# One decoder layer on one core: every second routed block fetched as quarter rows and transposed by VectorE instead of TensorE

## What is computed

```python
def body(acc, blk):                     # blk: 128 tokens that go to expert e, their weights
    toks, bw, e = blk
    xb = hp[toks]                       # hp: the 2048 rows, and a row of zeros for padding
    yb = (jax.nn.silu(xb @ w_gate[e]) * (xb @ w_up[e])) @ w_down[e]
    return acc.at[toks].add(yb.astype(f32) * bw[:, None]), None
```

## Time and profile before

| | us |
|---|---|
| median of 3 runs | 2494.95 |
| lowest, highest run | 2492.94, 2497.22 |
| the profiled execution, its own time | 2485.66 |
| its span (first to last instruction) | 2483.8 |
| TensorE busy in the span | 2382.5 (96%) |
| VectorE, ScalarE, GpSimd busy | 1575.5, 1161.9, 767.3 |
| mean granted TensorE clock | 0.985 |

### The profile page before, as it was taken

The page is one execution under the profiler, slowest core; times in us unless marked ns, Lnnn a source line. Parts: engine busy times, 40 slices in busy tenths (PEclk is TensorE's granted clock), DMA queues, the critical chain, the costliest instruction groups (busy, mean ns, idle before and its releaser), DMA issues. The chain is left out here.

```text
span 2483.8 us, 49979 instructions
## 1 busy us (share of the span) xinstructions
PE 2382.5 (96%) x11840; PEld 1954.7 (79%) x11842; DVE 1575.5 (63%) x2285; ACT 1161.9 (47%) x1621; POOL 767.3 (31%) x829
## 2 busy tenths in 40 slices
PE   8899999989997799999999999999999999999986
PEld 6677777678886688888888888888888888888875
DVE  6686867768878756555665555656665556655447
ACT  4525253542225645445554445545554445544334
POOL 0010100011110134334543433534443334444327
PEclk9999999989998899999999999999999999999998
DMA  7242323364445579778988878888888789987863
GB/s 254 77 144 98 111 94 111 117 218 164 171 164 206 196 230 284 223 219 270 273 259 233 254 218 263 268 266 262 257 253 243 224 223 274 283 247 222 216 221 136
DMA packets 253808, 524.34 MB, mean 211 GB/s; under 512 B 18065, under 2 KB 165169, under 8 KB 249649
## 3 DMA queue, kind: packets, MB, share of 16 engines
q1 hardware_dynamic: 204464, 336.64, 39.7%
q0 software_dynamic: 48672, 186.86, 29.4%
q10 hardware_dynamic: 608, 0.02, 0.0%
HBM read 386.61 MB, written 136.87 MB: 211 GB/s over the span
## 5 line engine op out<-in xcount | busy, mean ns | idle before, releaser
L2503 PE MATMUL psG<-gu_split,xT_hi 128*128 x2624 | 624.3, 390 | 2.9 <-ACT xT_hi L2340 1.5
L2503 PEld LDWEIGHTS psG<-gu_split,xT_hi 128*128 128x128 f32 x2624 | 493.8, 188 | 106.2 <-issue 3.6
L2326 POOL DMA_INDIRECT acc<-y,si x162 | 290.1, 1791 | 728.6 <-DMA acc<-y,si 413.3
L2409 DVE TENSOR_TENSOR gu_split<-raw_gu,gu_split (+1 forms) x127 | 290.6, 2288 | 175.3 <-ACT gu_split L2344 171.7
L2514 PE MATMUL psG<-gu_split,xT_lo 128*128 x1304 | 339.3, 402 | 5.9 <-issue 5.8
L2514 PEld LDWEIGHTS psG<-gu_split,xT_lo 128*128 128x128 f32 x1304 | 233.1, 188 | 50.1 <-issue 8.7
L2344 ACT ACTIVATE gu_split<-raw_gu x126 | 234.3, 1907 | 33.5 <-issue 33.5
L2301 POOL DMA_INDIRECT xg<-htab,gi x164 | 205.0, 1250 | 130.4 <-POOL gi L2298 109.7
L2409 DVE TENSOR_TENSOR d_lo<-raw_d,d_hi (+1 forms) x64 | 146.7, 2292 | 149.5 <-ACT d_hi L2344 149.5
L2389 ACT ACTIVATE HT_hi<-psH 128x256 fp32r<-128x256 f32 x162 | 62.4, 385 | 351.6 <-PE psH L2521 351.6
L2406 DVE TENSOR_TENSOR xT_lo<-psX,xT_hi 128x512 fp32r<-128x512 f32 x328 | 209.7, 680 | 8.5 <-ACT xT_hi L2340 8.5
(11 more groups left out here) (388 smaller groups left out, 3723.7 us busy)
## 6 DMA issues: line engine op xcount, KB each, us to landing
raw_gu<-in_w_gate_dram SPq DMA_DIRECT2D x64, 1024.0 KB, 6.0
raw_gu<-in_w_up_dram SPq DMA_DIRECT2D x64, 1024.0 KB
raw_d<-in_w_down_dram SPq DMA_DIRECT2D x64, 1024.0 KB, 6.9
wring<-split_d SPq DMA_DIRECT2D x24, 1024.0 KB, 4.8
split_d<-wring POOLq DMA_DIRECT2D x8, 1024.0 KB, 4.2
raw_d<-mixed SPq DMA_DIRECT2D x16, 512.0 KB, 3.9
xt<-in_x_dram SPq DMA_DIRECT2D x16, 512.0 KB, 4.3
htab<-h SPq DMA_DIRECT2D x16, 512.0 KB, 2.6
```

The lines of the kernel that those rows point to most:

```text
L2326: nc.gpsimd.indirect_dma_start(out=acc, out_offset=bass.IndirectOffsetOnAxis(ap=si[k][:, 0:1], axis=0), in_=y[k][:], in_offset=None, compu ...
L2409: nc.vector.tensor_tensor(dst, src, hi, ALU.subtract).then_inc(dlo_s if n == 2 else gulo_s, 1)
L2503: nc.tensor.matmul(psG[slot][:], xT_hi[slot][:, c, :], right[:, bass.ds(w, 1), c, :].rearrange("p a n -> p (a n)"), start=(n == 0 and c == ...
```

## The change

Blocks with an even number go the old way, through one row gather and 8 TensorE transposes. Blocks with an odd number go a new way.

- A second table `hcut` in HBM holds the same rows cut in four pieces of `PIECE` = 272 values (256 features, 16 expert weights; 1088 bytes). `output_and_route` writes both tables: one more store of 512 KB per tile, and for each pair of tiles two more stores of weights in runs of 64 bytes; `place_and_share` writes 4 more stores of zeros. Waits on these stores count them (32 for 16, 48 for 16).
- An odd block is gathered by 4 indirect DMAs of 128 pieces each, so that partitions 32a to 32a+31 hold piece a. The piece numbers `pidx` come from 16 new small VectorE instructions in `indices`.
- VectorE turns the block in squares of 32x32 with two instructions (128x1024 and 128x128) into `xF` in SBUF. ScalarE and VectorE take the high and low part from there in one instruction each instead of two. The expert weights of the block are turned once more by one TensorE transpose (`turn_weights`) into `psW`, from which `pairw` is copied.
- Chunk c now holds features 8q+c for both kinds of blocks. Gate and up weights are loaded to match, and TensorE's transposes of even blocks read `xg` with a step of 8 values (32 bytes) between columns.
- The copies into `gi` and `si` move from GpSimd to ScalarE (`gather_index`, `scatter_index`).

The diff, cut to its core:

```diff
             def store_h(n):
                 sp.wait_ge(h_s, n + 1)
                 sp.dma_start(htab[n * P:(n + 1) * P, 0:D], h[n % 2][:]).then_inc(row_out[n % 2], 16)
+                sp.dma_start(hcut[n * P:(n + 1) * P, :, 0:FEATS], h[n % 2][:].rearrange("p (a w) -> p a w", a=QUADS)).then_inc(row_out[n % 2], 16)
...
+                for i in range(w):
+                    sp.dma_start(hcut[(t + i) * P:(t + i + 1) * P, :, FEATS:PIECE],
+                                 wrow[r % 2][:, i, :].rearrange("p (a e) -> p a e", a=QUADS)).then_inc(wt_out[r % 2], 16)
...
+def gather_pieces(nc, hcut, to, at, done):
+    for g in range(QUADS):
+        nc.gpsimd.indirect_dma_start(out=to[:, g, 0:PIECE], out_offset=None, in_=hcut.rearrange("r a w -> (r a) w"),
+                                     in_offset=bass.IndirectOffsetOnAxis(ap=at[:, g:g + 1], axis=0)).then_inc(done, 16)
...
+                dve.wait_ge(idx_s, 2)
+                odd = idx[:].rearrange("p (b k) -> p b k", k=2)[:, :, 1]
+                for a in range(QUADS):
+                    for g in range(QUADS):
+                        last = nc.vector.tensor_scalar(pidx[a * QP:(a + 1) * QP, :, g], odd[g * QP:(g + 1) * QP], float(QUADS), float(a),
+                                                       ALU.mult, ALU.add)
+                last.then_inc(idx_s, 1)
...
-                        sp.dma_start(dst, w[0, bass.ds(e, 1)].rearrange("a (k p) n -> p (a k) n", p=P)).then_inc(sm, 16)
+                        rows = "a (k p) n -> p (a k) n" if sm is down_in else "a (p k) n -> p (a k) n"
+                        sp.dma_start(dst, w[0, bass.ds(e, 1)].rearrange(rows, p=P)).then_inc(sm, 16)
...
                 for n, s, k in steps(i):
-                    pool.wait_ge(turned[1], s.n + 3)
-                    pool.wait_ge(pairw_s, s.n + 3)
+                    pool.wait_ge(next_gi_s, s.n + 1)
+                    if k == 0:
+                        pool.wait_ge(pairw_s[0], s.turn + 2)
                     carry_wait(pool, passed)
-                    gather(s.n + AHEAD, k, s.n + AHEAD + 1)
-                    nc.gpsimd.tensor_copy(si[k][:], idx[:, bass.ds(s.n, 1)]).then_inc(si_s, 1)
+                    if k:
+                        gather_pieces(nc, hcut, xg[1], gi[1], x_in[1])
+                    else:
+                        gather_rows(nc, htab, xg[0], gi[0], x_in[0])
...
+            def turn_x(nth):
+                dve.wait_ge(x_in[1], nth * 16 * QUADS)
+                if not (isinstance(nth, int) and nth == 1):
+                    dve.wait_ge(odd_wturn, nth - 1)
+                    dve.wait_ge(odd_xhi, nth - 1)
+                carry_wait(dve, passed)
+                nc.vector.transpose(xF[:, 0:KC, :].rearrange("p c (g j) -> p c g j", g=QUADS),
+                                    xg[1][:, :, 0:FEATS].rearrange("p g (i c) -> p c g i", c=KC))
+                nc.vector.transpose(xF[:, KC, :].rearrange("p (g j) -> p g j", g=QUADS),
+                                    xg[1][:, :, FEATS:WIDE]).then_inc(odd_turned, 1)
...
                     s.wait(dve, H_s)
-                    pair_weight(nexts[n + 1], k, s.turn + 2)
-                    product(s.n + 2, 1 - k)
+                    if k == 0:
+                        pair_weight(nexts[n + 1], s.turn + 2, 0)
+                        pair_weight(nexts[n], s.turn + 1, 1)
+                    product(s.n + 2, 1 - k, s.turn + 1 + k)
+                    if k == 0:
+                        turn_x(s.turn + 2)
                     when_first(dve, nexts[n + 1], lambda: split(nexts[n + 1], 0))
...
+                rows = xg[0][:, 0:D].rearrange("p (q c) -> p c q", c=KC)
                 for h in range(2):
+                    if not (isinstance(nth, int) and nth == 1):
+                        pe.wait_ge(xlo_s[h], nth - 1)
+                    for c in range(HALF):
+                        m = nc.tensor.transpose(psX[h][:, c, :], rows[:, h * HALF + c], ident[:])
+                    m.then_inc(turned[h], 1)
...
                     turn_H(1 - k)
-                    pe.wait_ge(x_in[1 - k], (s.turn + k + 2) * 16 )
-                    carry_wait(pe, passed)
-                    for h in range(2):
-                        pe.wait_ge(xlo_s[h], s.n + 3)
-                        turn_x(1 - k, h)
+                    if k:
+                        turn_weights(s.turn + 2)
+                        turn_x(s.turn + 3)
...
+            def high_x(nth, slot):
+                if slot:
+                    act.wait_ge(odd_turned, nth)
+                    nc.scalar.activation(xT_hi[1][:], xF[:, 0:KC, :], ACT.Copy).then_inc(odd_xhi, 1)
+                    return
```

More of the change, by code:

```diff
@@ L2175, in experts @@
         xlo_s = [sem(f"xlo_s{i}") for i in range(2)]
-        pairw_s = sem("pairw_s")
+        odd_turned = sem("odd_turned")
+        odd_wturn = sem("odd_wturn")
+        odd_xhi = sem("odd_xhi")
+        odd_xlo = sem("odd_xlo")
+        next_gi_s = sem("next_gi_s")
+        pairw_s = [sem(f"pairw_s{i}") for i in range(2)]
         dhi_s = sem("dhi_s")
@@ L2206, in expert, with column @@
                 return within(self.word & (EXPERTS - 1), 0, EXPERTS - 1)
+            def column(self):
+                share = EXPERTS // QUADS
+                return within((self.word & (EXPERTS - 1)) + (self.word & (EXPERTS - share)), 0, P - 1)
             def next(self):
@@ L2296, in _ @@
         def _(pool):
[L2297 to L2307 removed]
+            for k in range(2):
+                if k == 0:
+                    pool.wait_ge(turned[1], 1)
+                    pool.wait_ge(pairw_s[0], 1)
+                    nc.gpsimd.tensor_copy(gi[0][:], idx[:, 2:3]).then_inc(gi_s, 1)
+                    pool.wait_ge(gi_s, 3)
+                    gather_rows(nc, htab, xg[0], gi[0], x_in[0])
+                else:
+                    pool.wait_ge(odd_turned, 1)
+                    nc.gpsimd.tensor_copy(gi[1][:], pidx[:, 1, :]).then_inc(gi_s, 1)
+                    pool.wait_ge(gi_s, 4)
+                    gather_pieces(nc, hcut, xg[1], gi[1], x_in[1])
             for k in range(2):
@@ L2446, in _ @@
             split_first(1)
-            for h in range(2):
-                evac_x(h, 1, 0)
+            low_x(1, 0)
             split_first(2)
-            pair_weight(block0, 0, 1)
-            pair_weight(block1, 1, 1)
+            for k in range(2):
+                dve.wait_ge(acc_out[k], 16 * EARLY // 2)
+            pair_weight(block0, 1, 0)
+            dve.wait_ge(tails_s, 1)
+            turn_x(1)
             when_first(dve, block0, lambda: split(block0, 0))
-            product(1, 0)
-            for h in range(2):
-                evac_x(h, 2, 1)
+            product(1, 0, 1)
+            low_x(1, 1)
             when_first(dve, block0, lambda: split(block0, 1))
@@ L2483, in _, with turn_x, turn_weights, gate_up_high @@
         def _(pe):
-            def turn_x(slot, half):
-                for c in range(HALF):
-                    m = nc.tensor.transpose(psX[half][:, c, :], xg[slot][:, (half * HALF + c) * P:(half * HALF + c + 1) * P], ident[:])
-                m.then_inc(turned[half], 1)
-            def gate_up_high(nth, slot, entry):
-                for h in range(2):
-                    pe.wait_ge(xhi_s[h], nth)
+            def turn_x(nth):
+                pe.wait_ge(x_in[0], nth * 16)
+                carry_wait(pe, passed)
+                rows = xg[0][:, 0:D].rearrange("p (q c) -> p c q", c=KC)
+                for h in range(2):
+                    if not (isinstance(nth, int) and nth == 1):
[3 more added lines that the diff above has]
+                    m.then_inc(turned[h], 1)
+            def turn_weights(nth):
+                pe.wait_ge(odd_turned, nth)
+                if not (isinstance(nth, int) and nth == 1):
+                    pe.wait_ge(pairw_s[1], nth - 1)
+                carry_wait(pe, passed)
+                nc.tensor.transpose(psW[:], xF[:, KC, :], ident[:]).then_inc(odd_wturn, 1)
+            def gate_up_high(nth, slot, entry, seen):
+                if slot:
+                    pe.wait_ge(odd_xhi, seen)
+                else:
+                    for h in range(2):
+                        pe.wait_ge(xhi_s[h], seen)
                 pe.wait_ge(gulo_s, entry.rank() * 2)
@@ L2505, in gate_up_high, with gate_up_low @@
                                          start=(n == 0 and c == 0), stop=False)
-            def gate_up_low(nth, slot, entry):
-                for h in range(2):
-                    pe.wait_ge(xlo_s[h], nth)
+            def gate_up_low(nth, slot, entry, seen):
+                if slot:
+                    pe.wait_ge(odd_xlo, seen)
+                else:
+                    for h in range(2):
+                        pe.wait_ge(xlo_s[h], seen)
                 w = entry.slot()
```

175 lines of the change are left out of this document (100 added, 75 removed).

## The result

The change made the kernel slower: 2598.93 us (median of 4 runs, 2595.07 to 2603.21) against 2493.94 for the kernel before on the same chip (2487.02 to 2497.22). The ratio is 1.0425, 95% interval 1.0396 to 1.0454. The prediction was 2452, range 2435 to 2512.

The account below looks back on a forecast made before the run. TensorE's own work was taken as the bound, transfers second. 57 us saved less charges of 5, 3, 3 and 3 gave 43 off 2485.66: 2442.7, or 2452 as the median of runs; range 2435 to 2512.

Parts of the forecast that it names:

- What goes: TensorE in odd blocks: 8 transposes go, one comes; 0.70 us a turn, 57 us over 81 turns.
- the charges of 5, 3 and 3: Expected losses in the loop: 5 us for H's shorter cover, 3 for quarter gathers, 3 for denser transfers.
- The strided read: TensorE's weight loads in even blocks, step of 32 bytes: taken as no change; upper end 0.80 us more a block.
- its rival: Strided weight loads in even blocks run at half rate: 65 us back, 2517 us, range 2495 to 2530; chance 0.17.
- VectorE's turns: VectorE's transposition of odd blocks: 1.5 us, upper end 3.0, fitting into 2.77 us of idle time; cost nothing.
- The shorter cover for H: After even steps TensorE reaches the down product 0.80 us sooner and may wait for `HT_lo`; 5 us charged.
- Transfers and small packets: Transfer engines in the expert stage: pieces of 1088 bytes add 0.16 us of share a turn, taken as nothing.
- The rival of dear packets: Small indirect packets in odd blocks' gathers cost as large ones: 165 us slower, 2660 us; chance 0.04.
- ScalarE's copies: Two tiny index copies a step on ScalarE, 0.2 us each: nothing; without cover 65 us.
- Before the loop: Second-table stores, weight stores and index instructions ahead of the expert loop: 3 us in sum, bounds 1 and 6.
- Quarter gathers: GpSimd's four piece gathers in odd blocks: not the bound, pieces in time with about 1 us spare; 3 us charged.
- late pieces: VectorE waits for pieces behind stretched issues and a lagging scatter chain: 2503 us at worst, 2480 middle; chance 0.12.

Follow-up runs that it names:

- both: The changed kernel with one gather of whole rows for odd blocks and VectorE's transposition reading runs of 32 values: 2449.86 us, ratio 0.9837.
- layout: The kernel before with gate and up weights in the new feature order and TensorE's transposes of all blocks reading columns 32 bytes apart: 2490.6 us, ratio 1.0006.
- apart: The changed kernel with odd blocks' scatters into a second table and no scatter waiting for the one before: 2464.86 us, ratio 0.9903.
- four_short: The changed kernel with an odd block's four gathers fetching 32 whole rows each instead of 128 quarter rows: 2617.11 us, ratio 1.0518.
- tables: The kernel before with the stores into `hcut` and their waits added, and nothing that reads it: 2494.05 us, ratio 1.0024.
- one_gather: The changed kernel with an odd block fetched by one indirect DMA of 128 whole rows instead of four of quarter rows: 2462.3 us, ratio 0.9887.
- copies: The kernel before with only the copies of `gi` and `si` moved to ScalarE: 2485.87 us, ratio 0.999.
- spread: The changed kernel with two of the four pieces issued in the even step ahead of its scatter, two in the odd step: 2503.08 us, ratio 1.006.
- early: The changed kernel with all four pieces issued in the even step, ahead of its scatter: 2594.31 us, ratio 1.0436.
- spread_contig: The changed kernel with two pieces issued in each step and VectorE's transposition reading runs of 32 values: 2491.08 us, ratio 1.001.

## Why the prediction was wrong

**What goes: right.** With the four issues out of the way and VectorE's read contiguous (the kernel both) the loop is 42.8 us shorter; 57 less the charges of 5, 3 and 3 inside the loop was 46, though one of the 3 was for the quarter gathers, which that kernel doesn't have. The transposes start as foretold: eight at 1516.44, low matmuls at 1517.26, 0.82 us later, for 0.80 in the earlier trace rows.

**The strided read: right, and its rival refuted.** The weight load itself did get longer, 193 ns in place of 140 (first the changed kernel's, then the one before's; shortest, median, longest):

```profile
L2592 PEld LDWEIGHTS psX<-ident,xg x664: 185/193/230, 863.5 to 2495.2; 128*128 128x128 f32 x166
```

```profile
L2487 PEld LDWEIGHTS psX<-ident,xg x1320: 138/140/231, 852.8 to 2383.8; 128*128 128x128 f32 x189
```

but eight transposes still pass in 0.82 us, and layout, where every block's weight load takes 193 ns, stands at 1.0006. The same stride on VectorE costs 74%, 2.16 us for 1.24. The Trainium skill (Advanced Engine Details and Errata, SBUF Cachelines) says that another line for each access costs a penalty, without a size. Both lengths agree with it: here it is 0.05 us a load on TensorE, hidden, and 0.9 us an instruction on VectorE, not hidden.

**VectorE's turns at nothing: mis-sized.** 2.16 + 0.27 = 2.4 us lay between the 1.5 taken and the upper end of 3.0, but the 2.77 us of idle time didn't cover them in every turn. 0.91 us less in each turn gave 12 us with one gather or spread pieces and 24 in the changed kernel.

**The shorter cover for H: a little low.** 5 us was the charge. TensorE never waited for `HT_lo` before; it waits 7.5 us in 9 waits in the kernel both, 16.8 in 21 in apart and 21.5 in 28 in the changed kernel.

**Transfers and small packets: nothing, as taken.** The rival of dear packets fell with four_short and with a DMA share that fell to 0.82. ScalarE's copies cost nothing, as taken.

**Before the loop: perhaps mis-sized.** 3 us, at most 6, was the charge. The second table alone costs 1 to 11 us of the median (tables). The profiles can't size it better: the loop begins 11.9 us later in the changed kernel, 2.1 in one_gather, which does the same ahead of it but for its row numbers, and 7.0 in copies, which has neither table nor index instructions. Those are 0.25 us each, over 4.4 us.

**Quarter gathers: the step that failed.** "GpSimd issues 5 gathers and 2 scatters a turn: 5 x 1.25 + 2 x 1.79 = 9.8 us of 17.9, so it isn't the bound" took GpSimd's busy time for its hold on the turn. Three things in it were off.

First, the run of four. The prediction took 4 x 1.01 = 4.0 us. From the start of the first piece to the end of the fourth it is 4.7 us undisturbed and 6.0 on the mean (67 runs from 1000 to 2350 us), up to 8.3. Each issue is followed by 0.30 us, and one beside a VectorE split takes 2 to 3 us in place of 0.95: the fourth piece at 1515.88 took 3.05 beside a split from 1515.81, the first two of the next turn 3.01 and 2.45 beside those from 1531.49 and 1534.30. The prediction had the row for this and charged 3 us. In those 67 runs 56 of the 268 pieces took more than 1.8 us, and all 56 ran beside a VectorE instruction with two SBUF inputs, a split or the low part of an odd block; of the other 212 34 did. The Trainium skill's note that GpSimd contends with VectorE instructions of two SBUF inputs (GPSIMD Engine Reference, Key points) agrees with this trace.

Second, the landing. It took 3 to 4 us; the piece in the timeline took 5.7, the one case that was looked at.

Third, and this is the cause that apart shows, the scatters. 413 us of GpSimd waiting for its own scatters was read as a sign that GpSimd has time to spare. But a scatter that waits for the landing of the one before is part of a loop of its own, and in the kernel before about half of the scatters were released by it, on the mean 9.77 us after the one before, where a step took 9.34. There was little room, and TensorE's saving of 0.35 us a step could be had only if this loop got shorter too. It could, as the kernel both shows with 9.0 us and the wait in place. Instead each turn put four issues into one of its two links: the even scatter waits for a landing, the pieces wait behind it in GpSimd's order and so come late to VectorE, and the odd scatter waits behind the pieces or for a landing that has itself become later. In the changed kernel's trace a turn is so 10.44 + 9.63 = 20.1 us for 18.7. Take away the landing's wait (apart) or halve the run (spread), and 134 or 96 us come back. Move the run as a whole (early), and nothing does. Of the 147 us between the forecast of 2452 and the 2598.93 measured, 134 so hang on the wait and the run of four together: taking away either is enough (apart 134, one_gather 137), and apart's 2464.86 lies within the predicted range. VectorE's step, worth 12 us from one_gather to both and from spread to spread_contig, is the size of what is left, though the two weren't joined in one run.

The rival "late pieces" named the right queue and the "lagging scatter chain", but priced it as lateness against VectorE's deadline, 1 us in two of three turns, 2503 at the worst. It didn't let the delay add to itself from scatter to scatter.

**The clock.** The same window of both kernels, the one before first:

```profile
1000.00:2300.00 1300.00, 1294.96 (x6408) 1086.38 (x6407) 756.57 (x1003) 647.28 (x863) 541.08 (x557) 1.00 0.86 250
```

```profile
1000.00:2300.00 1300.00, 1213.72 (x5492) 979.42 (x5492) 846.54 (x998) 616.88 (x996) 640.74 (x453) 0.96 0.82 233
```

TensorE is idle for 86 us of 1300, where it was for 5; over the 1612.8 us of the loop that makes 107. The loop should have shrunk to 1513.3 - 57 = 1456 with 6 us idle, and has 157 more. So some 101 of these are idle time, and the rest, 56, is busy time grown longer while the granted clock fell from 1.00 of 2.4 GHz to 0.96, in an engine that now stops for up to 4.6 us. That the stops lowered the clock is argued from this alone; with the waits gone, apart shows 1.00 again from 1400 to 1600 us.

## What to carry to other kernels

An engine that waits for its own transfers doesn't thereby have time to spare: count how many of its waits a landing ends, and add up one link of that chain (issue, landing, next issue) against the step, before anything is put between two links. The chain's mean period won't tell, since it follows the step. Here an indirect DMA cost GpSimd about a microsecond for each instruction, with 32 rows as with 128, and often two to three beside VectorE's two-input work; if several are needed, try to spread them over the steps. When an engine's wait is taken away and the time stays, look where the wait went.

## What the runs showed of the hardware

- An indirect gather of 128 pieces of 1088 bytes took GpSimd 0.95 us undisturbed, one of 32 whole rows 0.86, one of 128 whole rows 0.99, and 0.30 us went by before the next.
- VectorE's 32x32 transposition of 128x1024 float32 took 1.24 us in runs of 32 values and 2.16 with a step of 32 bytes; a TensorE weight load with that step took 193 ns for 140, without any effect on the pace of the transposes.
- In 1000 to 2200 us the gathers' and scatters' queue needed as much transfer time per MB with quarter rows as with whole ones: 43.0% of 16 engines for 129.28 MB, against 45.9% for 140.72 MB in one_gather, which is 64 and 63 us of engine time per MB.
- Of 268 issues of quarter rows, 56 took more than 1.8 us, 2.5 on the mean; all of them ran beside a VectorE instruction with two SBUF inputs.
- In the changed kernel the scatters landed later: 9.0 us in the median against 7.5 in the kernel before, over 1000 to 2300 us. One_gather had 8.8, so the run of small gathers isn't the whole reason, and what is stays open.
